# Stick-breaking attention: scores of the two heads of a pair issued alternately, softplus steps per head, the high and low split on GpSimd, output copies on VectorE

## The reference

```python
def stick_breaking_attention(q, k, v):      # 16 heads of 64, SEQ = 256
    ...
        z = jnp.einsum('bthd,bshd->bhts', qt, k).astype(jnp.float32) * scale
        strict = s_idx[None, :] < t[:, None]
        log_beta = jax.nn.log_sigmoid(z)
        log_1mb = jnp.where(strict, log_beta - z, 0.0)
        after = lax.cumsum(log_1mb, axis=3, reverse=True) - log_1mb
        a = jnp.where(strict, jnp.exp(log_beta + after), 0.0)
        o = jnp.einsum('bhts,bshd->bthd', a.astype(v.dtype), v)
```

## Time and profile before

| what | us |
|---|---|
| median of 3 runs | 703.39 |
| lowest, highest | 703.31, 705.05 |
| the profiled execution | 703.38 |
| its span in the trace | 701.5 |
| PE busy | 679.7 |
| DVE, ACT, POOL busy | 437.8, 367.3, 131.8 |

### The profile page before, as it was taken

One profiled execution on the slowest core, in us unless ns is written; L12 is line 12 of the kernel. 1 busy time (PEld: TensorE's weight loads), 2 busy tenths in 40 slices (PEclk: granted clock), 3 DMA queues, 4 the chain that ended last, 5 costly groups with the idle time before them and its releaser, 6 DMA issues.

```text
span 701.5 us, 11316 instructions
## 1 busy us (share of the span) xinstructions
PE 679.7 (97%) x4357; PEld 599.6 (85%) x4359; DVE 437.8 (62%) x564; ACT 367.3 (52%) x499; POOL 131.8 (19%) x85
## 2 busy tenths in 40 slices
PE   4989999999999999999999999999999999999996
PEld 3878887778799999998887999777789999998885
DVE  4577775577776666756447554575775757575532
ACT  5555425475466464746334633497474646466320
POOL 0022220000123434342001000000004343444000
PEclk9999999999999999999999999999999999999999
DMA  8947643002364445454752745300645353634601
GB/s 335 397 158 276 220 168 120 1 2 66 116 239 181 185 173 198 161 209 177 263 191 69 291 173 189 120 1 4 236 151 213 147 221 137 231 132 180 235 1 60
DMA packets 18652, 116.21 MB, mean 166 GB/s; under 512 B 2463, under 2 KB 3133, under 8 KB 5693
## 3 DMA queue, kind: packets, MB, share of 16 engines
q1 hardware_dynamic: 17325, 111.52, 42.9%
q10 hardware_dynamic: 1296, 4.26, 1.8%
HBM read 114.72 MB, written 1.05 MB: 165 GB/s over the span
## 4 chain that ended last, share of the span: by engine, by line
PE 87%; issue 4%; DVE 3%; ACT 3%; POOL 2%; DMA 1%; DVEq 0%; POOLq 0%; ACTq 0%
PE ps L1127 23%; PE ps L1129 23%; PE ps L1128 23%; PE ps L1169 3%; PE ps L1317 2%; PE ps L1504 1%; PE ps L1243 1%; PE ps L1277 1%; POOL rstd L1056 1%; PE ps L1122 1%; PE ps L1253 1%; DVE xn L650 1%; PE ps L1519 1%; ACT whi L329 1%; PE ps L1403 1%
## 5 line engine op out<-in xcount | busy, mean ns | idle before, releaser
L621 DVE TENSOR_TENSOR wlo<-raw,whi 128x2048 fp32r<-128x2048 f32 x99 | 226.8, 2320 | 73.3 <-ACT whi L329 73.3
L329 ACT CAST whi<-raw 128x2048 fp32r<-128x2048 f32 x99 | 186.0, 1917 | 69.3 <-PE ps L1129 67.2
L1127 PE MATMUL ps<-xhi,whi 128*128 128x256 f32 x768 | 217.9, 284 | 0.0
L1129 PE MATMUL ps<-xhi,wlo 128*128 128x256 f32 x768 | 217.7, 283 | 0.0
L1128 PE MATMUL ps<-xlo,whi 128*128 128x256 f32 x768 | 217.7, 283 | 0.0
L1127 PEld LDWEIGHTS ps<-xhi,whi 128*128 128x128 f32 x768 | 147.7, 192 | 0.0
L1128 PEld LDWEIGHTS ps<-xlo,whi 128*128 128x128 f32 x768 | 147.7, 192 | 0.0
L1129 PEld LDWEIGHTS ps<-xhi,wlo 128*128 128x128 f32 x768 | 147.6, 192 | 0.0
L513 ACT ACTIVATE conv<-ps,c_conv 128x256 f32<-128x256 f32 x88 | 42.5, 563 | 101.7 <-PE ps L1129 100.2
L1096 POOL TENSOR_TENSOR hidf<-act_g,conv 128x512 f32<-128x512 f32 x22 | 74.1, 3370 | 83.7 <-ACT act_g L519 83.7
L953 DVE SCALAR_TENSOR_TENSOR conv<-ps,c_conv,conv 128x255 f32<-128x255 f32 x88 | 38.4, 478 | 77.4 <-ACT conv L513 76.9
(11 more groups left out here) (174 smaller groups left out, 813.1 us busy)
## 6 DMA issues: line engine op xcount, KB each, us to landing
raw<-in_weights SPq DMA_DIRECT2D x101, 1024.0 KB, 4.9
c_gpre<-in_gpre ACTq DMA_DIRECT2D x4, 512.0 KB, 4.8
raw<-in_weights SPq DMA_DIRECT2D x4, 512.0 KB, 8.3
c_gpost<-in_gpost ACTq DMA_DIRECT2D x4, 512.0 KB, 5.0
h<-in_x SPq DMA_DIRECT2D x2, 512.0 KB, 7.6
out<-h SPq DMA_DIRECT2D x4, 256.0 KB, 2.0
t<-in_masks SPq DMA_DIRECT2D x1, 512.0 KB, 14.4
c_rope<-in_rope SPq DMA_DIRECT2D x1, 256.0 KB, 14.2
```

Of the source, the lines that this page charges most:

```text
L329: act.copy(whi[:, slot, :], raw[:, slot, :]).then_inc(hi_done, 1)
L621: dve.tensor_tensor(wlo[:, slot, :], raw[:, slot, :], whi[:, slot, :].bitcast(F32), ALU.subtract).then_inc(lo_done, 1)
L1127: pe.matmul(out, s_hi, m_hi, start=start, stop=False, skip_group_check=shared)
L1129: return pe.matmul(out, s_lo, m_hi, start=False, stop=stop, skip_group_check=shared)
```

## The change

Scores: the two mask products of a pair go first and open the banks, then the products with the first 128 keys of head 0 and head 1, then those with the other 128 keys of head 0 and head 1. Minus_abs, Exp, Ln and softplus are issued per head (384 columns), twice as many instructions of half the size. The split in high and low parts leaves ACT and DVE and goes to POOL, per head, a cast and a subtraction that waits for the cast. Both output copies are on DVE. On ACT the Exp of pair n+2 stands between the two weights of pair n, and its two Ln behind them. On DVE softplus(n+1) and minus_abs(n+2) alternate by head, and the output copies follow. The sums wait per head.

```diff
--- before.py
+++ after.py
@@ -553,30 +553,20 @@
 
             ffn(0)
 
-            def sb_soft(n):
-
-                s = n % 3
-                act.wait_ge(sb_absd, n + 1)
-                act.activation(sb_sp[:, s], sb_sp[:, s], ACT.Exp).then_inc(sb_exp1, 1)
-                act.wait_ge(sb_exp1, n + 1)
-                act.activation(sb_sp[:, s], sb_sp[:, s], ACT.Ln, bias=1.0).then_inc(sb_ln, 1)
-
-            def sb_soft_hi(n):
-                act.wait_ge(sb_spd, n + 1)
-                if n >= 2:
-                    act.wait_ge(sb_cum, 2 * (n - 1))
-                act.copy(sb_sphi[:, n % 2], sb_sp[:, n % 3]).then_inc(sb_sph, 1)
-
-            def sb_weights(n):
+            def sb_exp(n, hd):
+
+                act.wait_ge(sb_absd, 2 * n + hd + 1)
+                act.activation(sb_sp[:, n % 3, hd], sb_sp[:, n % 3, hd], ACT.Exp).then_inc(sb_exp1, 1)
+
+            def sb_log(n, hd):
+                act.wait_ge(sb_exp1, 2 * n + hd + 1)
+                act.activation(sb_sp[:, n % 3, hd], sb_sp[:, n % 3, hd], ACT.Ln, bias=1.0).then_inc(sb_ln, 1)
+
+            def sb_weights(n, hd):
                 if n >= 2:
                     act.wait_ge(sb_pv, n - 1)
-                for hd in range(2):
-                    act.wait_ge(sb_cum, 2 * n + hd + 1)
-                    act.activation(sb_a[:, n % 2, hd], ps[:, sb_bank(n) + hd, 0:384], ACT.Exp).then_inc(sb_prob, 1)
-
-            def sb_hi(n):
-                act.wait_ge(sb_pv, n + 1)
-                act.copy(xhi[:, n, :], ps[:, 6 + n % 2, 0:SEQ]).then_inc(sb_ohi, 1)
+                act.wait_ge(sb_cum, 2 * n + hd + 1)
+                act.activation(sb_a[:, n % 2, hd], ps[:, sb_bank(n) + hd, 0:384], ACT.Exp).then_inc(sb_prob, 1)
 
 
             pre(2)
@@ -587,27 +577,31 @@
                     u += 1
                     if step == ("unit", 5, 0):
                         act.preload_act_table_set("natural_log_exp_and_others")
-                        sb_soft(0)
+                        for hd in range(2):
+                            sb_exp(0, hd)
+                        for hd in range(2):
+                            sb_log(0, hd)
                     if step[2] == 1:
                         c = step[1]
                         if c == 5:
-                            sb_soft(1)
-                            sb_soft_hi(0)
+                            for hd in range(2):
+                                sb_exp(1, hd)
+                            for hd in range(2):
+                                sb_log(1, hd)
                         if c in (0, 5):
                             act.wait_ge(unit_used, ODD_END["unit", c])
                             act.copy(vbuf[:, :, (c // 5) * BLK:(c // 5 + 1) * BLK],
                                      ps[:, 2 * (c % 2):2 * (c % 2) + 2, :]).then_inc(in_free_act, 1)
 
 
-            for n in range(NP + 1):
-                if n < NP:
-                    sb_weights(n)
-                if n + 1 < NP:
-                    sb_soft_hi(n + 1)
+            for n in range(NP):
+                for hd in range(2):
+                    sb_weights(n, hd)
+                    if n + 2 < NP:
+                        sb_exp(n + 2, hd)
                 if n + 2 < NP:
-                    sb_soft(n + 2)
-                if n >= 1:
-                    sb_hi(n - 1)
+                    for hd in range(2):
+                        sb_log(n + 2, hd)
             plain_stage("out1")
             post_squares(2, 0)
             ffn(1)
@@ -976,27 +970,26 @@
 
             ffn(0)
 
-            def sb_minus_abs(n):
-
-                z = ps[:, sb_bank(n):sb_bank(n) + 2, 0:384].bitcast(U32)
+            def sb_minus_abs(n, hd):
+
+                z = ps[:, sb_bank(n) + hd, 0:384].bitcast(U32)
                 dve.wait_ge(sb_z, n + 1)
                 if n >= 3:
-                    dve.wait_ge(sb_spl, n - 2)
-                dve.tensor_scalar(sb_sp[:, n % 3].bitcast(U32), z, 0x80000000, None, ALU.bitwise_or).then_inc(sb_absd, 1)
-
-            def sb_softplus(n):
-
-                sp = sb_sp[:, n % 3]
-                dve.wait_ge(sb_ln, n + 1)
-                dve.scalar_tensor_tensor(sp, ps[:, sb_bank(n):sb_bank(n) + 2, 0:384], 0.0, sp, ALU.max,
+                    dve.wait_ge(sb_spl, 2 * (n - 3) + hd + 1)
+                dve.tensor_scalar(sb_sp[:, n % 3, hd].bitcast(U32), z, 0x80000000, None,
+                                  ALU.bitwise_or).then_inc(sb_absd, 1)
+
+            def sb_softplus(n, hd):
+
+                sp = sb_sp[:, n % 3, hd]
+                dve.wait_ge(sb_ln, 2 * n + hd + 1)
+                dve.scalar_tensor_tensor(sp, ps[:, sb_bank(n) + hd, 0:384], 0.0, sp, ALU.max,
                                          ALU.add).then_inc(sb_spd, 1)
 
-            def sb_softplus_lo(n):
-                dve.wait_ge(sb_sph, n + 1)
-                dve.tensor_tensor(sb_splo[:, n % 2], sb_sp[:, n % 3], sb_sphi[:, n % 2].bitcast(F32),
-                                  ALU.subtract).then_inc(sb_spl, 1)
-
-            def sb_lo(n):
+            def sb_out(n):
+
+                dve.wait_ge(sb_pv, n + 1)
+                dve.tensor_copy(xhi[:, n, :], ps[:, 6 + n % 2, 0:SEQ]).then_inc(sb_ohi, 1)
                 dve.wait_ge(sb_ohi, n + 1)
                 dve.tensor_tensor(xlo[:, n, :], ps[:, 6 + n % 2, 0:SEQ], xhi[:, n, :].bitcast(F32),
                                   ALU.subtract).then_inc(sb_olo, 1)
@@ -1008,11 +1001,12 @@
                     split_ahead(u)
                     u += 1
                     if step == ("unit", 5, 0):
-                        sb_minus_abs(0)
-                        sb_softplus(0)
-                        sb_minus_abs(1)
-                    elif step == ("unit", 5, 1):
-                        sb_softplus_lo(0)
+                        for hd in range(2):
+                            sb_minus_abs(0, hd)
+                        for hd in range(2):
+                            sb_softplus(0, hd)
+                        for hd in range(2):
+                            sb_minus_abs(1, hd)
                     if step[1] in ODD_TILE and step[2] == 1:
                         c = step[1]
                         dve.wait_ge(unit_used, ODD_END["unit", c])
@@ -1022,17 +1016,16 @@
                                           SCALE if c % 2 else 1.0, None, ALU.mult).then_inc(turned_out, 1)
 
 
+            for hd in range(2):
+                sb_softplus(1, hd)
             for n in range(NP + 2):
-                if n + 1 < NP:
-                    sb_softplus(n + 1)
+                for hd in range(2):
+                    if 1 <= n and n + 1 < NP:
+                        sb_softplus(n + 1, hd)
+                    if n + 2 < NP:
+                        sb_minus_abs(n + 2, hd)
                 if n >= 2:
-                    sb_lo(n - 2)
-                if n + 1 < NP:
-                    sb_softplus_lo(n + 1)
-                if n == 0:
-                    sb_minus_abs(2)
-                if n + 3 < NP:
-                    sb_minus_abs(n + 3)
+                    sb_out(n - 2)
             plain_stage("out1")
             junction(2)
             ffn(1)
@@ -1109,6 +1102,20 @@
             pool.wait_ge(late_in, 16 * LATE)
             pool.wait_ge(gate_ready, 1)
             pool.tensor_copy(tri_r, c_tri[:]).then_inc(tri_cast, 1)
+
+            def sb_split(n, hd):
+
+                pool.wait_ge(sb_spd, 2 * n + hd + 1)
+                if n >= 2:
+                    pool.wait_ge(sb_cum, 2 * (n - 2) + hd + 1)
+                pool.tensor_copy(sb_sphi[:, n % 2, hd], sb_sp[:, n % 3, hd]).then_inc(sb_sph, 1)
+                pool.wait_ge(sb_sph, 2 * n + hd + 1)
+                pool.tensor_tensor(sb_splo[:, n % 2, hd], sb_sp[:, n % 3, hd], sb_sphi[:, n % 2, hd].bitcast(F32),
+                                   ALU.subtract).then_inc(sb_spl, 1)
+
+            for n in range(NP):
+                for hd in range(2):
+                    sb_split(n, hd)
             junction(2)
             ffn(1)
 
@@ -1498,23 +1505,25 @@
 
             def sb_scores(n):
                 for hd in range(2):
-                    rows, bank = slice(HD * hd, HD * hd + HD), sb_bank(n) + hd
+                    bank = sb_bank(n) + hd
                     if n >= 3:
                         pe.wait_ge(sb_prob, 2 * (n - 3) + hd + 1)
-                    pe.matmul(ps[:, bank, 0:SEQ], qkT[rows, NP + n, 0:P], qkT[rows, n, :], start=True, stop=False,
+                    pe.matmul(psq[:, 4 * bank:4 * bank + 3:2, :], c_identb[:],
+                              c_mask[:, NG:NG + 1, 0:P].to_broadcast([P, 2, P]), start=True, stop=False,
                               skip_group_check=True)
-                    pe.matmul(ps[:, bank, SEQ:SEQ + P], qkT[rows, NP + n, P:SEQ], qkT[rows, n, P:SEQ], start=False,
-                              stop=False, skip_group_check=True)
-                    ins = pe.matmul(psq[:, 4 * bank:4 * bank + 3:2, :], c_identb[:],
```

(10 more changed lines are left out.)

## The result

| kernel | median us | range, executions |
|---|---|---|
| before | 703.73 | 703.31 to 705.05, 4 |
| changed | 698.73 | 698.03 to 699.53, 4 |

The ratio is 0.9925, with an interval of 0.9911 to 0.9939: faster by 0.75%. The profiled execution of the changed kernel took 698.03 us (span 696.2), 5.35 less than the profiled execution before (703.38, span 701.5). The forecast was 698.6. The changed kernel's median stands between two executions of 698.0 to 698.1 and two of 699.4 to 699.5. That it comes within 0.1 us of the forecast is luck; on the lower level the forecast is 0.6 us too high.

What follows compares the result with a forecast made beforehand. PE's order of work was taken as the bound, ACT just below. First scores 3.7, less a 1.6 us stall, plus iterations 2.9, less tail 0.2, make 4.8 us saved: 703.4 to 698.6, range 697.0 to 701.8.

Steps and rivals of the forecast that it cites:

- Bound: In the stage, PE's order of work sets the time, 4.02 us an iteration, with ACT just below, busy for 3.65.
- Scores: On PE, two heads on different row groups run at once; a pair costs 1.07 us instead of 1.95, saving 0.88.
- (c): Rival: heads of the new scores run one after the other on PE; 703.0 us in all; chance 0.06.
- the predicted 0.64 + 0.21: On PE, a pair's score products: 0.64 us for the 256 columns and about 0.21 for the 128 columns.
- The split: On POOL, per head, cast 0.52 us, subtraction 1.01 and two hand-overs of 0.06: 1.65, ends 1.50 and 2.07.
- The price in case it had been longer: Rival: POOL paces the stage from 1.73 us a head, each 0.1 us more costing 1.2 us; chance 0.13.
- The iteration: Steady iterations take 3.3 us instead of 4.02, including PE's 0.1 to 0.2 wait for second weights; 2.9 saved over four.
- Rival (d): Waiting for the second weights costs 0.5 us more in each of four iterations; 700.6 us in all; chance 0.12.
- The gap: Between scores(2) and scores(3), PE stands 1.6 us because ACT's second weights of pair 0 queue behind Exp(2, 0).
- The tail: For n = 5 to 7, PE work is unchanged; 0.2 us given back as output blocks wait for pair 5's weights.
- The sum: Whole kernel: 3.7 - 1.6 + 2.9 - 0.2 = 4.8 us saved, from 703.4 to 698.6.
- Rival (b): DVE blocks POOL: subtraction 2.56 us by the factor 3.27/1.29, 3.2 a head, 716.0 in all; chance 0.07.

Runs made afterwards that it cites:

- e2: Changed kernel with the old order of scores on PE, one head after the other, mask last: 704.95 us, ratio 1.0008 to the kernel before.
- e1: Kernel before with only the new order of the scores on PE; softplus, split and output steps unchanged: 700.83 us, ratio 0.9961.
- e3: Changed kernel with both weights of pair 0 on ACT put before both Exp of pair 2: 698.89 us, ratio 0.9926.
- e8: Changed kernel with both weights before any Exp, both softplus before both minus_abs, and ACT rounding head 1 instead of POOL: 698.31 us, ratio 0.992.
- e5: Changed kernel with one extra POOL copy of 384 columns, never read, ahead of each head's cast: 702.93 us, ratio 0.9982.
- e6: Changed kernel with one extra DVE addition of two SBUF operands, 256 columns, per pair: one execution, 698.43 us.
- e7: Changed kernel with masks still first but score products ordered head 0, head 0, head 1, head 1: 699.74 us, ratio 0.9934.
- e9: Changed kernel run again without edit, side by side on one chip with the shared-rounding version: 699.87 us, ratio 0.9941.
- e10: Version with both weights before any Exp and ACT rounding head 1, run again beside the changed kernel: 697.32 us, ratio 0.9904.

## Why the prediction was right, point by point

**Bound.** Right. PE's order of work was the bound and ACT stood just below: e2 (no shorter scores, no gain) and e1 (ACT paces at 3.66 us) show both halves.

**Scores.** The mechanism was right, the heads do run at once, and (c) is out. The size was off: 1.18 us, not 1.07. The products took 0.85 in all, exactly the predicted 0.64 + 0.21, but the masks took 0.33 and not 0.22. The step that failed is the sentence that the 0.64 "already holds an entry and an exit". It was read from a row's start, and a row starts behind the change of mode ahead of it; the entry, about 0.11 us between masks and products, was in no term of the sum. It isn't a wait for another engine: scores(2), whose masks wait for no pair's weights, show the same 0.32 (451.20 to 451.52). The Trainium skill, "TensorEngine Tiling (Array Packing)", Key Properties, says that changing the mode drains the engine; 0.11 is what this kernel's rows show for it, and setting the rule aside was the mistake. The scores ahead of sums(0) saved 1.66 in place of 1.76. Scores(2) and scores(3) saved 1.72 in place of 1.93: e3 and e8, where PE doesn't stand between them, take 3.62 from sums(0) to sums(1) against 5.34 before.

**The split.** Right: 0.50 and 1.01 us against 0.52 and 1.01, hand-over 0.08 against 0.06. A head takes 1.53 in place of 1.65, because consecutive instructions overlap at their ends, which was the lower bound of 1.50. The price in case it had been longer was right too (e5).

**The iteration.** The number was right (3.29 against 3.3) for reasons that offset each other. Its 3.14 for PE was 0.15 short: 0.11 in the scores and 0.03 in the sums. The wait of 0.1 to 0.2 for the second weights isn't there: the rows of iteration 3 have no bracket. It is missed by little, as ACT's row shows:

```profile
463.37 0.48 ACT L569 ACTIVATE sb_a<-ps 128x384 f32<-128x384 f32 x1
```

The second weights end at 463.85, 2.17 us after the start of the sums, where 2.25 had been counted; the masks begin at 463.79, and the second of them needs these weights 0.1 later. In the whole stage the masks' weight loads waited for the weights' Exp twice:

```profile
PEld ps L1511 <- ACT sb_a L569: 1.7, 2, 1.6
```

One is the gap (1.6) and the other the 0.17 at scores(4), which may be the change of mode alone, since the same 0.17 stands before the masks of iteration 3 with no releaser. ACT was busy for 2.51 us and not 3.10, since its starts overlap. Rival (d) was a wait that doesn't come up here, by a margin under 0.1 us.

**The gap.** Right in place, cause and size: 1.66 us between the masks of scores(3), 1.38 of it idle. What it cost is 1.56 us (5.18 against the 3.62 of e3 and e8), against the predicted 1.6. Its removal, though, is worth less than that as long as the rest of the order stays (e3).

**The tail.** Wrong in sign, 0.65 us: 0.45 saved in place of 0.2 given back. Before, sums(6) and sums(7) had waited for the low part. PE's rows at sums(6), before:

```profile
476.42 0.40 PE L1129 MATMUL ps<-whi,xlo 128*128 128x512 f32 x1
477.08 0.44 PE L1519 MATMUL ps<-sb_sphi,wg_parts 128*128 128x384 f32 x1 [0.26 <-DVE sb_splo L996]
```

and after:

```profile
471.75 0.40 PE L1136 MATMUL ps<-whi,xlo 128*128 128x512 f32 x1
471.99 0.34 PE L1528 MATMUL ps<-sb_sphi,wg_parts 128*128 128x384 f32 x1
```

From the last product ahead to the sums it was 0.66 us and is 0.24, so 0.42 are won here; POOL is done in time. Sums(6) to sums(7) win 0.15 more, 0.10 of it in the sums themselves (1.29 to 1.19, from 477.08 to 478.37 and from 471.99 to 473.18), whose first load no longer waits. The predicted give-back exists too, 0.12 us: the output blocks wait for pair 5's weights, and start 0.44 after the last values group (470.05) where it was 0.32 (474.83 to 475.15). The weight load's row, after:

```profile
470.48 0.19 PEld L1134 LDWEIGHTS ps<-whi,xhi 128*128 128x128 f32 x1 [0.28 <-ACT sb_a L569]
```

So the term that was there was about right, and one was missing. The wait was the longer part of the 1.0 us in the earlier trace rows, which I read and did not follow to its place. A wait for a tile whose maker the change replaces should have had a term in the sum.

**The sum.** Predicted 3.7 - 1.6 + 2.9 - 0.2 = 4.8. By the same parts the trace has 3.38 - 1.56 + 2.98 + 0.45 = 5.25: the scores 0.3 short, the tail 0.65 the other way, and the rest within 0.1. The offset between these two is luck. Sums(7) stood at 475.49 against a predicted 475.7.

**Rival (b).** It didn't slow the changed kernel: all 16 subtractions keep 1.01 us. From scores(2) on, its DVE steps have at most one SBUF operand. The condition that the Trainium skill, "Advanced Engine Details and Errata", GPSIMD Details, puts (two SBUF inputs) agrees with e6. But ahead of sums(0) one of DVE's weight subtractions, with two SBUF operands, falls beside the split of pair 0, head 1, and no order between the two is set. In e5 DVE starts first:

```profile
447.03 2.28 DVE L615 TENSOR_TENSOR wlo<-raw,whi 128x2048 fp32r<-128x2048 f32 x1
447.24 2.95 POOL L1114 TENSOR_TENSOR sb_splo<-sb_sp,sb_sphi 128x384 fp32r<-128x384 f32 x1
```

DVE's step ends at 449.31, and POOL's 0.88 later, as if it stood for the rest of DVE's step. In the changed kernel POOL starts first, and DVE pays, with 2.48 where the median of these steps is 2.29:

```profile
444.68 1.02 POOL L1113 TENSOR_TENSOR sb_splo<-sb_sp,sb_sphi 128x384 fp32r<-128x384 f32 x1
445.37 2.48 DVE L615 TENSOR_TENSOR wlo<-raw,whi 128x2048 fp32r<-128x2048 f32 x1
```

The 3.27 against 1.29 of the earlier trace rows reads the same way: with 2.28 for one step, DVE's first ended at 77.04, and POOL's ended 1.15 later. So the prediction's factor 3.27/1.29 was the wrong form of the price. What these meetings cost is at most the rest of the step that began first. By that reading, and as an estimate, a subtraction beside a softplus step of 0.56 us would come to 1.01 + 0.56 = 1.57 and not 2.56, so the 716.0 was too high even for its own case.

## What to carry to other kernels

In this kernel the heads on separate row groups ran at once only with no full-array matmul between them: gather the masks at one end first, and count the change of tile mode, about 0.1 us here. Shortening the engine that bounds is worth what the next one allows (here 3.3 of 5.3 us alone), so find the second bound before the edit. When one engine's queue mixes a step that releases the bottleneck with one that waits for a longer chain, the releasing step goes first; then look for the same pair of steps one iteration on, where the wait will come up next.

## What the runs showed that was not expected

**Levels of 1.4 to 1.6 us.** Executions of one kernel on one chip fall on levels that go with the mean granted clock: before, 703.0 to 703.7 mostly at 0.999 and 704.8 to 705.1 mostly at 0.997, with 704.07 and 705.56 beside them; changed, 698.03 and 698.10 at 0.999 and 0.998, and 699.35 and 699.53 at 0.996. The profile of e2 caught one inside the stage:

```profile
456.59 0.70 PE L1511 MATMUL ps<-qkT 64*128 64x256 f32 x2 [0.52 <-ACT sb_a L569]
```

```profile
458.00:461.00 3.00, 3.00 (x15) 2.16 (x14) 1.34 (x3) 2.20 (x6) 2.83 (x4) 0.50 0.00 0
```

The first is from PE's timeline, the second a window, with the clock behind POOL's busy time. PE had stood for 0.52 us, and then was granted 0.50, the 1.2 GHz of its two levels, from 458 to 461. The sums in it took 2.11 us in place of 1.27 and the values 1.48 in place of 0.80: 1.5 us lost, the distance between the levels. e5 and e7 show the same after gaps of 1.38 and 1.39 us, but the changed kernel, e6 and e9 have the same gap with the clock at 1.00 behind it. e5, e8, e9 and e10 have such a stretch in layer 0, near 50 to 54 us, where nothing was edited, for instance e8 (PE's timeline and a window):

```profile
49.59 1.16 PE L1410 MATMUL ps<-c_identf,xn 128*128 128x128 f32 x8 [2.05 <-POOL xn L1085]
```

```profile
50.00:54.00 4.00, 4.00 (x16) 3.25 (x15) 2.05 (x2) 3.22 (x3) 0.00 (x0) 0.57 0.85 303
```

There too PE had stood, for 2.05 us, and the changed kernel has that gap with full clock behind it. So a gap can end in half clock and need not. Some kernels with an idle PE in the first two iterations have executions two levels or more above their lowest (e9: 698.06, 699.56, 701.28; e1: 700.04 and 704.27), while e8 and e10 stay within 1.7 us. But e7 and the first four executions of the changed kernel have the gap and stay within 2.1 us. What decides it is open. What follows is how to compare: a median of four executions can move by 1.5 us by the level alone, and lowest against lowest, or starts within the stage, are sharper.

**Both sides pay.** In the meeting of e6 POOL lost 0.21 and DVE 0.22 (0.63 against 0.41), and in the changed kernel a subtraction of weights on DVE took 2.48 us in place of 2.29 beside the split. A step on GpSimd can slow the VectorE step beside it, and the rows of GpSimd alone wouldn't show that.
